# Inputs laid out with channels on partitions, and the modulation as row products on VectorE

## The reference, cut to what matters

```
mod_x = silu(c) @ w_mod + b_mod          # six parts of 1024: sh1, sc1, g1, sh2, sc2, g2
mod_c = silu(c_ctx) @ w_mod + b_mod      # only its first two parts are used
hx = rms_norm(x, norm1) * (1 + sc1) + sh1;   hc the same of ctx with mod_c
rx, rgx, q, k, v, ga, gb = split(hx @ w_in);  rc, kc, vc from hc @ w_in
y  = sigmoid(ga) * (rglru(rx, rc, rgx) @ w_o_rnn) + sigmoid(gb) * (attention(q, k, v, kc, vc) @ w_o_attn)
x  = x + g1 * (y @ w_out)
hx2 = rms_norm(x, norm2) * (1 + sc2) + sh2
x  = x + g2 * conv_ffn(hx2);  return rms_norm(x, final)
```

## Time and profile before

| | |
|---|---|
| median of 3 runs | 1920.99 us (1910.5 to 1925.39) |
| the profiled execution | 1923.09 us, span 1921.2 us |
| mean granted clock of TensorE | 0.975 of full speed |
| busy share PE / DVE / ACT / POOL | 95% / 60% / 37% / 32% |
| first gate product of the recurrence starts at | 208.4 us |

### The profile page before, as it was taken

How to read it: one execution, slowest core, us unless ns; L and a number is a source line. 1 busy time by engine, 2 the same in 40 slices (tenths; PEclk the granted TensorE clock), 3 DMA queues, 4 the chain that set the end, 5 groups by cost and what they waited for, 6 DMA issues and landing times.

```text
span 1921.2 us, 23400 instructions
## 1 busy us (share of the span) xinstructions
PE 1823.0 (95%) x8520; PEld 1495.7 (78%) x8520; DVE 1156.4 (60%) x1243; ACT 709.3 (37%) x930; POOL 611.5 (32%) x286
## 2 busy tenths in 40 slices
PE   7789989999989978999999998999999999999997
PEld 2788878888868867877888785888888888888886
DVE  2956367766931477776111318999998988534423
ACT  3620366556610016776000213544444444312202
POOL 0524477677534455553454561000000000000000
PEclk9889889999989989999999999999999999999999
DMA  7686112111134520001222341322222223632312
GB/s 270 187 300 225 50 42 66 58 57 52 39 108 157 151 66 1 0 0 50 71 66 66 110 153 34 98 89 87 76 87 83 80 90 105 238 109 73 107 42 91
DMA packets 191790, 184.23 MB, mean 96 GB/s; under 512 B 10632, under 2 KB 170992, under 8 KB 189424
## 3 DMA queue, kind: packets, MB, share of 16 engines
q1 hardware_dynamic: 178176, 163.98, 26.2%
q10 hardware_dynamic: 13552, 19.40, 3.4%
HBM read 142.99 MB, written 35.13 MB: 93 GB/s over the span
## 4 chain that ended last, share of the span: by engine, by line
PE 72%; DVE 15%; issue 4%; ACT 3%; DMA 3%; POOL 2%; ACTq 1%; SPq 0%; DVEq 0%; POOLq 0%
PE acc L871 16%; PE acc L872 15%; PE acc L873 15%; PE gp L871 7%; PE gp L873 7%; PE gp L872 7%; DVE pt_lo L2082 2%; DVE smax L2052 2%; PE gp L908 1%; DMA qs<-qf 1%; DVE yq L2036 1%; DVE qs L2033 1%; ACTq L1523 1%; DMA t_scratch<-rt 1%; PE gp L998 1%
## 5 line engine op out<-in xcount | busy, mean ns | idle before, releaser
L871 PE MATMUL acc<-hx_hi,whi_both 128*128 128x512 f32 x704 | 276.9, 393 | 12.4 <-POOL wlo_both L713 4.8
L872 PE MATMUL acc<-hx_lo,whi_both 128*128 128x512 f32 x704 | 276.3, 392 | 0.0
L873 PE MATMUL acc<-hx_hi,wlo_both 128*128 128x512 f32 x704 | 275.8, 392 | 0.0
L711 POOL TENSOR_TENSOR whi_both<-wst,ones 128x1024 fp32r<-128x1024 f32 x65 | 176.8, 2721 | 293.6 <-PE acc L873 242.9
L713 POOL TENSOR_TENSOR wlo_both<-wst,whi_both 128x1024 fp32r<-128x1024 f32 x65 | 190.3, 2927 | 5.1
L871 PEld LDWEIGHTS acc<-hx_hi,whi_both 128*128 128x128 f32 x704 | 133.7, 190 | 41.6 <-POOL wlo_both L713 5.5
L873 PEld LDWEIGHTS acc<-hx_hi,wlo_both 128*128 128x128 f32 x704 | 133.4, 190 | 28.3
L872 PEld LDWEIGHTS acc<-hx_lo,whi_both 128*128 128x128 f32 x704 | 133.4, 189 | 26.9
L871 PE MATMUL acc<-T_hi,fac_hi 128*128 128x512 f32 x264 | 102.8, 389 | 0.3 <-DVE fac_lo L2233 0.3
L872 PE MATMUL acc<-T_lo,fac_hi 128*128 128x512 f32 x264 | 102.7, 389 | 0.0
L873 PE MATMUL acc<-T_hi,fac_lo 128*128 128x512 f32 x264 | 102.7, 389 | 0.0
(11 more groups left out here) (337 smaller groups left out, 4685.9 us busy)
## 6 DMA issues: line engine op xcount, KB each, us to landing
wst<-in_w_in SPq DMA_DIRECT2D x52, 512.0 KB, 4.1
wrest<-in_w_mod SPq DMA_DIRECT2D x8, 2048.0 KB, 10.2
wst<-in_w_up SPq DMA_DIRECT2D x26, 512.0 KB, 4.4
ffn_row_scratch<-ca SPq DMA_DIRECT2D x24, 512.0 KB, 2.6
wst<-in_w_down SPq DMA_DIRECT2D x32, 384.0 KB, 3.5
g_in<-ffn_row_scratch SPq DMA_DIRECT2D x24, 512.0 KB, 7.0
wup<-in_w_up SPq DMA_DIRECT2D x22, 512.0 KB, 4.8
wmod<-in_w_mod SPq DMA_DIRECT2D x8, 1024.0 KB, 12.6
```

What stands on the lines that cost most here:

```text
L711: nc.gpsimd.tensor_tensor(whi[s][:, 0:kc, :], wst[s][:, 0:kc, :], ones_of(kc), mult).then_inc(S["w_hi"], 1)
L871: mm(out_ap, w_h, x_h, start=first, stop=False)
L872: mm(out_ap, w_h, x_l, start=False, stop=False)
L873: return mm(out_ap, w_l, x_h, start=False, stop=last)
```

## The change

- **Layouts made on the host.** `x` and `ctx` are given transposed (`x_rows`, `ctx_rows`), the parameters as one tile (`columns`), and w_mod transposed, output channel on partitions (`mod_first` in 8 tiles of 1 MB, `mod_rest` in 8 groups of 2 MB). All transposes of inputs on PE, the copies out of them and the store of `xT_scratch` go; the residual reads `x_rows`.
- **Sums of squares by matmul.** ACT squares each chunk of `x`, 16 matmuls with `ones` sum over partitions, ACT takes the root, DVE the reciprocal in two halves; the same for `ctx` with 8 matmuls.
- **Modulation by chunk.** `modulation(k, e)` multiplies w_mod's rows with silu(c) laid along the free dimension, and sums in the same DVE instruction (`accum_out`): two instructions of 1024 and two small ones a chunk, for `x` (e = 0) and then for `ctx` (e = 1). Then DVE scales the chunk (`scaled`), ACT modulates and rounds, DVE takes the low part (`low_x`).
- **Four products paced by chunk.** R row 0, RG row 0 and both keys are accumulated together, chunk after chunk as these become ready, in all eight PSUM banks. Then come the context's sum of squares, the values for `x` (8 tiles), the context's values and keys, and the eight context products rc, ahead of `gate(0, 0)`.
- **The rest of the modulation in the merge stages.** ACT's queue reloads c (0.5 MB as a broadcast) and loads 8 pieces of 0.5 MB for g1 in the merge stage, and 6 groups of 2 MB in the output stage; DVE does 8 and 24 products of 1024 with `accum_out`. 64 matmuls (L998) and `racc` go.

```diff
+            for k in range(KC):
+                sp.dma_start(xraw[:, k, :], D["x_rows"][k]).then_inc(x_loaded[k], 16)
+
+            def load_mod(k):
+                sp.dma_start(wmod[k][:, :, :], D["mod_first"][k]).then_inc(wm_loaded[k], 16)
+
+            load_mod(0)
...
+            load_w(col(w_in, COL_R, 0), 0)
+            load_w(col(w_in, COL_RG, 0), 1)
+            for s in range(N_KV):
+                sp.dma_start(kraw[s][:, :, :], col(w_in, COL_K, s)).then_inc(kw_loaded[s], 16)
+            for k in range(1, KC - 1):
+                load_mod(k)
+            sp.dma_start(craw[:, :, :], D["ctx_rows"]).then_inc(S["ctx_loaded"], 16)
+            sp.wait_ge(S["kw_ready"], N_KV)
+            load_mod(KC - 1)
+            sp.dma_start(ident[:, :], D["ident"]).then_inc(S["late_loaded"], 16)
+            sp.dma_start(masks[:, :, :], D["masks"]).then_inc(S["late_loaded"], 16)
+            for n in range(2):
+                load_w(col(w_in, COL_V, n), W_V + n)
...
+            sp.wait_ge(S["mod_sum"], 2 * KC + 6)
...
+            def first_part(k, o):
+
+                if k == 0:
+                    if o < 2:
+                        pe.wait_ge(S["kw_ready"], o + 1)
+                    else:
+                        weights(o - 2)
+                    if o == 3:
+                        slot_read(pe, 0)
+                w_h, w_l = (kw_hi[o], kw_lo[o]) if o < 2 else (whi[o - 2], wlo[o - 2])
+                for h in range(2):
+                    last = three(first_out[o][:, HALF * h:HALF * (h + 1)], w_h[:, k, :], w_l[:, k, :],
+                                 hx_hi[:, k, HALF * h:HALF * (h + 1)], hx_lo[:, k, HALF * h:HALF * (h + 1)], k == 0, k == KC - 1)
+                if k == KC - 1:
+                    last.then_inc(S["k_full"] if o < 2 else S["acc_full"], 1)
+
+            for k in range(KC - 2):
+                pe.wait_ge(S["hx_lo_x"], k + 1)
+                for o in (2, 3, 0, 1):
+                    first_part(k, o)
+            for outs in ((2, 3), (0,), (1,)):
+                for k in (KC - 2, KC - 1):
+                    pe.wait_ge(S["hx_lo_x"], k + 1)
+                    for o in outs:
+                        first_part(k, o)
+
+            pe.wait_ge(S["k_read"], 1)
+            pe.wait_ge(S["sq_done"], KC + 1)
+            for k in range(KC):
...
+            def reload_row(e):
+                act.dma_start(crow[e][:, :], D["c"].to_broadcast([P, D_MODEL])).then_inc(S["row_loaded"], 16)
...
+            def load_g1(j):
+                if j >= 3:
+                    act.wait_ge(S["rest_acc"], j - 2)
+                act.dma_start(wg1[j % 3][:, :], in_rest[j // NG, :, j % NG, :]).then_inc(wr_loaded[j % 3], 16)
+
+            act.wait_ge(S["z_lo_s"], KC)
+            reload_row(0)
+            for j in range(3):
+                load_g1(j)
+            merge_gate(A_S4, 0, 0, None)
+            row_again(0)
+            for j in range(3, 6):
+                load_g1(j)
+            merge_gate(A_S4, 1, 1, (S["row_silu"], 1))
+            for j in range(6, KC):
+                load_g1(j)
...
+            def load_groups(g):
+                if g >= 5:
+                    act.wait_ge(S["rest_acc"], KC + NG * (g - 4))
+                act.dma_start(wgr[(g - 2) % 3][:, :, :], in_rest[g]).then_inc(wr_loaded[(g - 2) % 3], 16)
...
+            full(act, A_S4 + 15)
+            reload_row(1)
+            for g in range(2, 5):
+                load_groups(g)
+            row_again(1)
             for m in range(KC - 1):
                 slot_read(act, A_S5 + m)
+                if 1 <= m < 4:
+                    load_groups(m + 4)
                 if m:
...
+            def modulation(k, e):
+
+                n = 2 * KC * e + 2 * k
+                if e == 0:
+                    dve.wait_ge(wm_loaded[k], 16)
+                for j in range(2):
+                    if n + j:
+                        dve.wait_ge(S["mod_sum"], n + j)
+                    v.scalar_tensor_tensor(out=junk[:, :], in0=wmod[k][:, j, :], scalar=1.0, in1=silu[e][:, :], op0=mult, op1=mult,
+                                           accum_out=msum[:, e, j, k:k + 1]).then_inc(S["mod_sum"], 1)
+                dve.wait_ge(S["mod_sum"], n + 2)
+                bias = pcol[:, C_BMOD:C_BMOD + 2 * KC].rearrange("p (j k) -> p j k", j=2)
+                v.tensor_tensor(mod[:, e, :, k:k + 1], msum[:, e, :, k:k + 1], bias[:, :, k:k + 1], add).then_inc(S["mod_add"], 1)
+                dve.wait_ge(S["mod_add"], KC * e + k + 1)
+                v.scalar_tensor_tensor(out=mod[:, e, 1, k:k + 1], in0=mod[:, e, 1, k:k + 1], scalar=1.0,
+                                       in1=pcol[:, C_N1 + k:C_N1 + k + 1], op0=add, op1=mult).then_inc(S["mod_ready"], 1)
+
...
+            scaled(0)
+            for k in range(1, KC):
+                modulation(k, 0)
+                scaled(k)
+                low_x(k - 1)
+            low_x(KC - 1)
+            dve.wait_ge(S["silu_ready"], 2)
+            for k in range(3):
+                modulation(k, 1)
+            dve.wait_ge(S["c_root"], 1)
+            v.reciprocal(rstd_c[:, :], rstd_c[:, :]).then_inc(S["rstd_done"], 1)
+            dve.wait_ge(S["rstd_done"], 3)
+            v.tensor_tensor(craw[:, :, :], craw[:, :, :], rstd_c[:, :].rearrange("p (o n) -> p o n", o=1).to_broadcast([P, KC, CTX]),
...
+            for k in range(3, KC):
+                modulation(k, 1)
+                if k == KC - 2:
+                    low_context(0)
+            low_context(1)
...
+            def add_rest(j, row, src, e, count):
+                dve.wait_ge(wr_loaded[e], WR_AT + count)
+                if j:
+                    dve.wait_ge(S["rest_acc"], j)
+                v.scalar_tensor_tensor(out=src, in0=src, scalar=1.0, in1=row, op0=mult, op1=mult,
+                                       accum_out=rest[:, j // KC, j % KC:j % KC + 1]).then_inc(S["rest_acc"], 1)
+
+            def add_g1(j):
+                add_rest(j, crow[0][:, :], wg1[j % 3][:, :], j % 3, 16 * (j // 3 + 1))
+
+            def add_group(g):
+                s, before = (g - 2) % 3, (16 * 3, 16 * 3, 16 * 2)[(g - 2) % 3]
+                for a in range(NG):
+                    add_rest(NG * g + a, crow[1][:, :], wgr[s][:, a, :], s, before + 16 * ((g - 2) // 3 + 1))
+
+            def rest_bias(a0, a1):
...
             low(hx_lo, yq, hx_hi, "mg_hi", "mg_lo", KC - 1)
             dve.wait_ge(S["mg_lo"], KC)
+            dve.wait_ge(S["rest_ready"], 1)
+            row_product(1)
             for m in range(KC):
+                if m < 6:
+                    add_group(m + 2)
+                elif m == 6:
+                    dve.wait_ge(S["rest_acc"], 4 * KC)
+                    rest_bias(1, 4)
+                    dve.wait_ge(S["rest_ready"], 2)
+                    link(v.scalar_tensor_tensor(out=a2col[:, :], in0=rest[:, 2, :], scalar=1.0, in1=pcol[:, C_N2:C_N2 + KC],
+                                                op0=add, op1=mult))
                 slot, last = (A_S5 + m) % 2, m == KC - 1
                 dve.wait_ge(xr_loaded[m % 2], 16 * (m // 2 + 1))
                 for h in range(2 if last else 1):
...
```

More of the change, by code:

```diff
@@ L960, in _ @@
[L960 to L967 removed]
+            pe.wait_ge(S["consts_set"], 2)
+            for k in range(KC):
+                pe.wait_ge(S["sq_done"], k + 1)
+                for h in range(2):
+                    last = mm(acc[0][:, HALF * h:HALF * (h + 1)], ones[:, :], xsq[:, k, HALF * h:HALF * (h + 1)],
+                              start=k == 0, stop=k == KC - 1)
@@ new lines, in _ @@
+            for k in range(KC - 2):
[9 more added lines that the diff above has]
+            pe.wait_ge(S["sq_done"], KC + 1)
+            for k in range(KC):
+                last = mm(gp[:, 0:CTX], ones[:, :], csq[:, k, :], start=k == 0, stop=k == KC - 1)
@@ L968, in _, with values @@
+            last.then_inc(S["c_sum"], 1)
+            def values(o, x_h, x_l, c0):
                 for k in range(KC):
@@ new lines, in scaled, with low_x @@
+            def scaled(k):
+                v.tensor_tensor(xraw[:, k, :], xraw[:, k, :], rstd_x[:, :], mult).then_inc(S["xs_done"], 1)
+            def low_x(k):
+                dve.wait_ge(S["hx_hi_x"], k + 1)
+                v.tensor_tensor(hx_lo[:, k, :], xraw[:, k, :], hx_hi[:, k, :], sub).then_inc(S["hx_lo_x"], 1)
+            silu_row(0)
+            silu_row(1)
+            dve.wait_ge(S["silu_ready"], 1)
+            modulation(0, 0)
+            for h in range(2):
+                if h == 0:
+                    dve.wait_ge(S["x_root"], 1)
+                else:
+                    dve.wait_ge(acc_read[0], 1)
+                part = slice(HALF * h, HALF * (h + 1))
+                v.reciprocal(rstd_x[:, part], rstd_x[:, part]).then_inc(S["rstd_done"], 1)
@@ L1865, in taps, with low_context @@
+            def low_context(half):
+                part = slice(KQ * half, KQ * (half + 1))
+                dve.wait_ge(S["hx_hi_c"], half + 1)
```

(15 more changed lines are left out.)

648 lines of the change are left out of this document (281 added, 367 removed).

## The result

The changed kernel takes 1896.93 us (median of 4 runs, 1887.85 to 1898.04) against 1920.86 for the kernel before on the same chip: ratio 0.9884, 95% interval 0.9853 to 0.9916. It is 1.2% faster, by half of what was forecast, and lies just above the range. Its profiled execution took 1898.04 us with a span of 1896.3; the sum of the prediction, made against such an execution, was 1875.6.

The account below looks back on a forecast made before the run. PE was taken to bound the kernel, busy 1823 of 1921 us. 1923.1 - 52 (opening) + 1 (first recurrence step) + 3.5 (output stage) = 1875.6; with the profiled run 2 us above the median, 1874 was predicted, range 1853 to 1896.

Parts of the forecast that it names:

- The small ones are not served one for one: Output stage: small weight packets beside the groups' large ones get perhaps a third of the rate.
- the 2.5 us for late weights: Output stage: POOL's split begins 2.5 us later beside the group loads, and PE waits that long.
- The bound of 10 us for this: Output stage: upper bound on the late-weights wait, if small runs had to wait out four of the six MB.
- Squares and root keep pace behind the loads of x: Opening: x's sum of squares adds no delay after the loads; first tile there at 19 to 20 us.
- POOL's four low parts lie under the reciprocals: Opening: POOL's four low parts, 2.35 us each, lie under DVE's one-input reciprocals, 6.7 us.
- The lag of the output stage: Output stage: DVE and POOL need 12.2 us a product against PE's 10.9; mostly absorbed, cost 1, bounds 0 and 6.
- rival 1: Slower: `accum_out` costs two passes, 2.57 us, delaying opening and output stage; 1931 us, chance 0.05.
- The wait for `hc_lo`: Opening, ahead of the context's values: PE waits some 4 us for the context's low parts.
- a cost of 1: First step of the recurrence, after the gate: POOL's weight splits cost 1 us, at most 4.8.
- 2: Rival: output stage pays more, by starved weights (10), unabsorbed lag (6) and a late first group (5); 1892 us, chance 0.17.
- 3: Rival: opening 14 us late by slower transfers, longer half clock and the context's wait behind ACT; 1889 us, chance 0.15.
- 4 to 5 us for half clock: Four products of the opening: PE, idle before, runs some 10 us at 1.2 GHz, costing 4 to 5 us.

Follow-up runs that it names:

- The run with the high parts first: Changed kernel with ACT rounding the first two weight pieces' high parts ahead of the root of the sum of squares: 1893.63 us, 0.9877 of the kernel before.
- the first combined version: Changed kernel plus early output-stage weights, ACT's high parts there, both sums of squares in one pass, high parts ahead of the root: 1870.39 us, 0.9758.
- the sum in one pass: Changed kernel with the squares of x and the matrix of ones in f32r instead of f32: 1890.35 us, 0.9865 of the kernel before.
- the best version: Changed kernel plus early output-stage weights, ACT's high parts there and both sums of squares in one pass, the root ahead of the opening's high parts: 1868.78 us, 0.9726.

## Why the prediction was wrong

The sign and the mechanism were right, and two terms of the sum were not. Against 1875.6 the profiled run had 22.4 us more: 8.0 from the opening, 17.1 from the output stage, 0.3 behind it, less 3.0 that the steps between gave.

**"The small ones are not served one for one" failed; this is the larger part.** It was the step on which the 2.5 us for late weights stood, and it rested on counts over 8 us, 1040 small packets against 88 large ones. Those counts mix two stretches. In the same trace, at 106 to 107 us:

```profile
q1 hardware_dynamic: 25, 0.34, 81.0%
q10 hardware_dynamic: 23, 0.01, 3.9%
```

and at 107 to 108, where the large ones had run out:

```profile
q10 hardware_dynamic: 580, 0.30, 97.9%
q1 hardware_dynamic: 12, 0.00, 0.7%
```

One for one while both have work, then the small ones alone. The window was wider than the overlap, and the store landed in 5.2 us because its company was short, not because it had a third of the rate. In the output stage the company is 6 MB: POOL's first split there was forecast at 1078 - 50 + 2.5 = 1030.5 us and came at 1050.38. The bound of 10 us for this was too low as well: it let the small runs wait out four of the six MB, where at 3% of the bytes they wait out all six, less what had gone before: the wait was 20.1. The runs with the groups delayed (wait 7.5 in three pieces), in 4 KB rows (12.7) and with the weights ahead (3.8 for low parts) show it from three sides.

The Trainium skill ("DMA: Bandwidth & Descriptors", section "Queues, rings and completion order") says that each DMA engine takes turns between queues packet by packet, with some 9 to 17 descriptors in a packet as a rule. The trace agrees on turns of equal number, 143 to 143; what the profile counts as one packet here holds 0.5 or 14.5 KB, and whether that is the page's packet no run here shows.

**"Squares and root keep pace behind the loads of x" failed.** The sentence gives the 16 calls of the sum no price; at the price of the rounded type they would keep pace, but they came at 1.01 us a call. The row for it was there: L908's 64 records in the earlier trace rows are 32 calls in the code, 29.8 us, so 0.93 us each. I read 64 as calls. This is 4.5 us, and shown: in the rounded type the reciprocals start at 23.35. The context's sum, 2 us in the sum, took 3.6. The Trainium skill ("FP8 and Floating Point Precision", section "TensorE Precision Notes") gives true FP32 four passes through the array; 1.01 against 0.227 us, 4.4 times, is near that.

**"POOL's four low parts lie under the reciprocals" failed too, only in part with it.** By the prediction's own numbers 4 x 2.35 = 9.4 us cannot lie under 6.7. ACT had the weights queued behind the late root, and DVE paid as in the earlier trace rows (3.41 us for 1.22 there, 3.01 and 3.38 here): 3.9 us. With the root in time 1.5 of them go, and 2.4 stay (1.51 and 3.37), as the last key lands at 27.6 us and its low part ends behind the reciprocals. The run with the high parts first has both at 1.22 and the gate 4.1 earlier.

**The lag of the output stage, "cost 1", was under-priced but not charged.** DVE and POOL need the 12.2 us worked out. In the changed kernel the 20 us stop hid it: from the second residual to the last it took 65.2 us, as before. Where the stop is gone it costs 6 to 7.5 us, the upper bound of 6 or above it, and by another path than the one priced: with early weights PE waits for no bank, but for POOL's low parts of the weights, for which the prediction had no term.

**Right.** Alone, the row products with `accum_out` cost 1.22 us and 0.08 for reading the sum, 1.28 in the forecast; so rival 1 falls, and with it, here, the rule of the Trainium skill ("Vector Engine (DVE) Microarchitecture Reference", "Points that are easy to get wrong") that two SBUF inputs that aren't bf16 halve this form. The wait for `hc_lo` was 3.5 us (4 forecast), the waits for rc's low parts 3.8 in all, and from first product to gate it took 119.7 us for a forecast of 120. The merge stage cost nothing. From the gate to the queries 1.2 us was gained where a cost of 1 was charged; its waits (3.9 for `glo`, 2.9 for weights) are those of before, 3.9 and 3.1.

**The rivals.** 2 named the output stage and both its mechanisms, 3 a late opening. Each was priced as if the other did not happen, 1892 and 1889; what came was the first mechanism of 2 at twice its price and 8 of 3's 14 us, for other reasons. The range ended where one of them ends. The version that mends what failed has the gate at 156.6, by a forecast of 156.5, and takes 1868.8 us, 5 less than 1874. That the gates meet is in part luck: 2.4 us of the collision are still in it, while PE's granted clock stayed at 1.00 where the forecast charged 4 to 5 us for half clock, and the context's sum was made cheaper than in the kernel forecast.

## What to carry to other kernels

Before a large load is put beside a small one that is waited for, compare the sizes of their packets, in a window in which both queues have work: with one packet for one, 0.5 KB runs beside 16 KB rows get 3% of the bytes; issue the small ones first, or cut the large rows. Count the calls in the code against the records in the trace before a price per record is taken, above all for f32 products. And when DVE gets new work with two SBUF inputs, add up DVE and POOL as if they were one engine, and move POOL's instructions to ACT where it has room: here that, with a later place for the weights of the second product, was worth about as much as leaving the work out.

## What the hardware showed unasked

**The exclusion of DVE and POOL alternates by whole instructions.** While both have work in the queue, a DVE product of 1.22 us takes 3.2 and POOL's 2.35 takes 3.2 to 3.4. The rows fit turns of one instruction each (the changed kernel's output stage, DVE then POOL): POOL's first ends at 1074.62, DVE's product 1.1 us behind it at 1075.70, POOL's next 2.3 us behind that at 1077.96, DVE's next 1.1 us later at 1079.05.

```profile
1072.48 3.22 DVE L2131 SCALAR_TENSOR_TENSOR wgr<-wgr,crow 128x1024 f32<-128x1024 f32 x1
1075.64 0.08 DVE L2131 DVE_READ_ACCUMULATOR wgr<-wgr,crow 128x1 f32 x1
1075.82 3.23 DVE L2131 SCALAR_TENSOR_TENSOR wgr<-wgr,crow 128x1024 f32<-128x1024 f32 x1
```

```profile
1071.37 3.25 POOL L687 TENSOR_TENSOR wlo_both<-wst,whi_both 128x1024 fp32r<-128x1024 f32 x1
1074.58 3.38 POOL L822 TENSOR_TENSOR ssum<-ssum,sqb 128x1024 f32<-128x1024 f32 x1
```

**An idle PE was not always granted 1.2 GHz.** Ahead of the first product PE stood for 17.7 us in the changed kernel and 20.0 in the first combined version. The clock from 30 to 40 and 40 to 50 us was 0.62 and 0.53 in the one, and in the other it stayed whole (PE's busy time in these 10 us, the other engines, clock):

```profile
30.00:40.00 10.00, 0.00 (x0) 0.00 (x0) 9.86 (x11) 3.30 (x3) 3.42 (x2) 1.00 1.01 420
40.00:50.00 10.00, 9.85 (x34) 7.96 (x35) 9.79 (x17) 4.45 (x5) 0.00 (x0) 1.00 1.06 375
```

The nearest pair is the sum in one pass and the best version, whose sums of x are the same: PE stood for 18.5 us in both, and the clock from 20 to 40 us was 0.50 in the first and 1.00 in the second. What makes the difference no run here shows.
